# First expert stage of a decoder layer: the gate-weighted one-hots of the first key are built on GpSimd instead of VectorE

## The reference, cut to what matters

```python
q = jnp.einsum('td,dhq->thq', xt, w_pq)                # 8 heads, two halves of 128
v1, i1 = lax.top_k(q[..., :half] @ keys1.T, 16)        # first key
v2, i2 = lax.top_k(q[..., half:] @ keys2.T, 16)        # second key
sc, ci = lax.top_k(v1[..., :, None] + v2[..., None, :], 16)
eid = i1[ci // 16] * 128 + i2[ci % 16]                 # 128 experts a token: 8 heads x 16
gate = softmax(sc)
hid = gelu(xt @ expert_u[eid])
out = (gate * hid) @ expert_v[eid]
```

## Time and profile before

| | |
|---|---|
| Median of 3 runs | 2118.77 us (2118.34 to 2120.36) |
| Span of the profiled execution | 2115.7 us |
| Median less span | 3.1 us |
| TensorE busy | 2016.0 us, 95% |
| VectorE busy | 1619.7 us, 77% |
| GpSimd busy | 552.0 us, 26% |
| Mean granted TensorE clock | 0.979 of full speed |

### The profile page before, as it was taken

How to read it: one execution, slowest core, us unless ns; L and a number is a source line. 1 busy time by engine, 2 the same in 40 slices (tenths; PEclk the granted TensorE clock), 3 DMA queues, 4 the chain that set the end, 5 groups by cost and what they waited for, 6 DMA issues and landing times.

```text
span 2115.7 us, 33945 instructions
## 1 busy us (share of the span) xinstructions
PE 2016.0 (95%) x12943; PEld 1845.7 (87%) x12943; DVE 1619.7 (77%) x3030; ACT 794.0 (38%) x1311; POOL 552.0 (26%) x334
## 2 busy tenths in 40 slices
PE   8998889889999999999999999999989899999998
PEld 8998879778756999999999999999978787778786
DVE  6635767564355327999999799999979888989888
ACT  4335453432331322322344444444433333333332
POOL 0000020000000000212112055555547656656540
PEclk9999889999999999999999999999999999999999
DMA  5223210151550403768667488999999999999993
GB/s 171 89 93 116 86 47 1 41 204 42 191 208 21 160 1 121 261 232 285 223 219 270 140 290 330 338 346 340 337 381 387 386 387 387 383 385 384 375 377 113
DMA packets 223185, 483.75 MB, mean 229 GB/s; under 512 B 11984, under 2 KB 137168, under 8 KB 221415
## 3 DMA queue, kind: packets, MB, share of 16 engines
q1 hardware_dynamic: 176998, 314.56, 41.9%
q0 software_dynamic: 46080, 167.79, 21.8%
HBM read 423.29 MB, written 58.36 MB: 228 GB/s over the span
## 4 chain that ended last, share of the span: by engine, by line
PE 43%; DMA 8%; DVE 5%; SPq 3%; issue 1%; ACT 1%; DVEq 0%; ACTq 0%
PE ps L2599 9%; PE ps L2595 9%; PE ps L2991 8%; PE ps L2594 8%; DMA raw_v<-peer_v 6%; PE ps L2585 5%; PE ps L2623 4%; SPq L2969 3%; DVE kept L3100 3%; DVE v_high_low L3163 1%; DVE outputs L3157 1%; DMA outputs<-hidden 1%; ACT v_high_low L3057 0%; DMA kept<-peer_v,kept 0%; SPq L2967 0%
## 5 line engine op out<-in xcount | busy, mean ns | idle before, releaser
L2991 PE MATMUL ps<-v_high_low,gated_high_low 128*128 128x512 f32 x2304 | 532.9, 393 | 22.0 <-ACT gated_high_low L3059 18.3
L2991 PEld LDWEIGHTS ps<-v_high_low,gated_high_low 128*128 128x128 f32 x2304 | 435.8, 190 | 119.0 <-ACT v_high_low L3057 15.0
L2594 PE MATMUL ps<-x_high_low,u_high_low 128*128 128x384 f32 x1024 | 356.3, 348 | 0.0
L2595 PE MATMUL ps<-x_high_low,u_high_low 128*128 128x384 f32 x1024 | 345.6, 337 | 0.0
L3083 POOL DMA_INDIRECT outputs<-peer_v,kept x138 | 264.2, 1914 | 170.0 <-DVE kept L3100 137.3
L2711 POOL DMA_INDIRECT scores<-peer_u,kept x64 | 94.0, 1468 | 729.3 <-DVE kept L2831 552.4
L2669 ACT ACTIVATE kept<-ps 128x384 f32<-128x384 f32 x128 | 62.9, 491 | 407.5 <-PE ps L2599 398.0
L2599 PE MATMUL ps<-x_high_low,u_high_low 128*128 128x384 f32 x1024 | 204.7, 341 | 0.0
L2595 PEld LDWEIGHTS ps<-x_high_low,u_high_low 128*128 128x128 f32 x1024 | 193.3, 189 | 0.0
L2594 PEld LDWEIGHTS ps<-x_high_low,u_high_low 128*128 128x128 f32 x1024 | 193.0, 189 | 0.0
L3163 DVE TENSOR_TENSOR v_high_low<-raw_v,v_high_low 128x1024 fp32r<-128x1024 f32 x120 | 146.3, 1219 | 51.1 <-ACT v_high_low L3057 51.1
(11 more groups left out here) (471 smaller groups left out, 4113.9 us busy)
## 6 DMA issues: line engine op xcount, KB each, us to landing
experts<-peer_u SPq DMA_DIRECT2D x63, 1024.0 KB
raw_v<-peer_v SPq DMA_DIRECT2D x60, 1024.0 KB
hidden<-kept SPq DMA_DIRECT2D x64, 384.0 KB
gates<-scores SPq DMA_DIRECT2D x12, 2048.0 KB, 9.4
first_hidden<-hidden SPq DMA_DIRECT2D x16, 768.0 KB, 18.4
outputs<-gates SPq DMA_DIRECT2D x16, 768.0 KB
outputs<-hidden SPq DMA_DIRECT2D x16, 768.0 KB, 15.4
first_gates<-gates SPq DMA_DIRECT2D x15, 768.0 KB
```

Of the source, the lines that this page charges most:

```text
L2594: pe.matmul(o, utr[:, b, HI, k], xr[:, HI, k, 0:DN], start=(k == 0), stop=False)
L2595: pe.matmul(o, utr[:, b, HI, k], xr[:, LO, k, 0:DN], start=False, stop=False)
L2991: ins = pe.matmul(bank(c, 2 * t + h), gr[:, slot, x, DN * b + P * t:DN * b + P * t + P], vr[:, slot, y, D * b + 512 * h:D * b + 512 * h + ...
```

## The change: what it does

The `gated` one-hots leave VectorE. GpSimd makes them, one token to an instruction: a `tensor_scalar` of 128 x 128 elements that compares the row of key numbers with the token's first keys and multiplies by the token's gates, both taken as one value per partition. That is 8 instructions for each octet, 384 in all, where VectorE had 2 for each octet, 96 in all. VectorE keeps the one comparison for `hot2`. TensorE waits for both before an octet's first call. GpSimd's gathers are no longer asked for as soon as the ring allows: ahead of octet `o` it asks for those that the ring allows after the dot products of octet `o - 2`. The number of dot products that VectorE makes after octet `o` now comes from `dots_after(o)`, which rounds down where the old expression rounded up.

```diff
+OCTETS = NTG * QG // 2
+
+def dots_after(o):
+
+    return DOTS_BY[2] if o < 0 else min(ROWSETS, DOTS_BY[2] + (ROWSETS - DOTS_BY[2]) * (o + 1) // (OCTETS + 3))
...
                 if first == 0:
                     pe.wait_ge(hot_set, tg * (QG // 2) + (i // 2 + 1))
+                    pe.wait_ge(gated_hot_set, tg * (QG // 2) + (i // 2 + 1))
...
-            for no in range(ROWSETS):
-                i = no % RING
-                if no == PAIRS_EACH:
-                    pool.wait_ge(ids_set, 2)
-                after(pool, row_used, no - RING + 1)
-                pool.indirect_dma_start(out=ring[i], out_offset=None, in_=d.peer_u[0],
-                                        in_offset=bass.IndirectOffsetOnAxis(ap=ids[:, no:no + 1], axis=0)).then_inc(row_in[i], 16)
+            asked = [0]
+
+            def gather(upto):
+                for no in range(asked[0], min(upto, ROWSETS)):
+                    i = no % RING
+                    if no == PAIRS_EACH:
+                        pool.wait_ge(ids_set, 2)
+                    after(pool, row_used, no - RING + 1)
+                    pool.indirect_dma_start(out=ring[i], out_offset=None, in_=d.peer_u[0],
+                                            in_offset=bass.IndirectOffsetOnAxis(ap=ids[:, no:no + 1], axis=0)).then_inc(row_in[i], 16)
+                asked[0] = max(asked[0], min(upto, ROWSETS))
+
+            gather(DOTS_BY[2] + RING)
+            pool.wait_ge(gates_set, 1)
+            for o in range(OCTETS):
+                gather(dots_after(o - 2) + RING)
+                slot = o % 2
+                after(pool, made, 2 * (o - 1))
+                for t in range(OCT):
+                    at, cols = OCT * o + t, slice(P * t, P * t + P)
+                    ins = pool.tensor_scalar(gated[slot][:, cols], iota, kt[:, 0, at:at + 1], kt[:, 3, at:at + 1], ALU.is_equal, ALU.mult)
+                ins.then_inc(gated_hot_set, 1)
+            gather(ROWSETS)
...
-            before, octets = dots[0], NTG * QG // 2 + 3
-            for o in range(NTG * QG // 2):
+            for o in range(OCTETS):
                 t0, slot = OCT * o, o % 2
                 after(v, made, 2 * (o - 1))
-                keys, k2 = over(iota, 1, [P, OCT, NK]), hot2[slot].rearrange("p (t k) -> p t k", t=OCT)
-                k1 = gated[slot].rearrange("p (t k) -> p t k", t=OCT)
-                v.tensor_tensor(k1, keys, over(kt[:, 0, t0:t0 + OCT], 2, [P, OCT, NK]), ALU.is_equal).then_inc(hot_first, 1)
-                v.tensor_tensor(k2, keys, over(kt[:, 1, t0:t0 + OCT], 2, [P, OCT, NK]), ALU.is_equal)
-                v.wait_ge(hot_first, o + 1)
-                v.tensor_tensor(k1, k1, over(kt[:, 3, t0:t0 + OCT], 2, [P, OCT, NK]), ALU.mult).then_inc(hot_set, 1)
+                v.tensor_tensor(hot2[slot].rearrange("p (t k) -> p t k", t=OCT), over(iota, 1, [P, OCT, NK]),
+                                over(kt[:, 1, t0:t0 + OCT], 2, [P, OCT, NK]), ALU.is_equal).then_inc(hot_set, 1)
                 if lows[0] < NK:
                     low()
-                while dots[0] < min(ROWSETS, before - (before - ROWSETS) * (o + 1) // octets):
+                while dots[0] < dots_after(o):
                     dot()
```

More of the change, by code:

```diff
@@ L2503, in phase_hidden @@
         "tile_picked", "pairs_turned", "pairs_turned_out", "gate_exps", "gate_sums", "gates_set"))
-    hot_set, hot_first, made, gkept = s("gated_one_hots_set"), s("first_one_hots_set"), s("gates_made"), s("gates_kept")
+    hot_set, gated_hot_set, made, gkept = s("one_hots_set"), s("gated_one_hots_set"), s("gates_made"), s("gates_kept")
     xs_in, ids_set, exp_s, gelu_s = s("sample_x_in"), s("expert_ids_set"), s("gathered_gate_exps"), s("gathered_gelu")
```

## The result

The changed kernel takes 2317.19 us (median of 4 runs, 2315.87 to 2324.20) against 2118.56 us for the kernel before (4 runs, 2118.05 to 2120.36). The ratio is 1.0943, with a 95% interval of 1.0927 to 1.0959: 9.4% slower. The profiled execution took 2315.87 us, with a span of 2314.1 us against 2115.7 us, 198.4 us more. Forecast were 2121 us, within 2113 to 2208.

The account below looks back on a forecast made before the run. TensorE was taken to set the pace at 6.87 us a row; 2115.7 - 0 + 0 + 2.4 = 2118.1 us of span, with 3.1 us between span and median 2121 us, 0.1% over before. The range was 2113 to 2208 us.

Parts of the forecast that it names:

- So 0.31 us is the work and the rest is waiting: GpSimd's 128-column additions in another stage, shown as 0.90 and 0.78 us: 0.31 us work, the rest waiting for VectorE.
- eight are 2.7 us: GpSimd's eight one-hots of an octet, at 0.34 us each, take 2.7 us a row.
- the additions show next to no fixed cost: Argument against dearer one-hots: GpSimd's additions take 1.27 us for 512 columns and 0.31 for 128.
- The sum for GpSimd's row: Gathers 3.96 us plus one-hots 2.7 us make 6.7 us a row, under TensorE's 6.87 by 0.2 us.
- The first octet: Tightest octet: between gates set and TensorE taking it, 5.2 us are left for 2.7 us of one-hots.
- The prediction is wrong if GpSimd's row passes 6.87 us: Stated condition for failure: GpSimd's work per row exceeds TensorE's row of 6.87 us; equality at 0.36 us for each one-hot.
- A one-hot costs more than 0.36 us: Rival, 29%: dearer one-hots on GpSimd give 2152 us at 0.45 us each, 2208 at 0.60, 2276 at 0.78.
- Turns: Rival, 21%: GpSimd shut out during VectorE's three two-input instructions, 3.42 us; its row 8.0 us, total 2175 us.
- The rule that speaks against it: VectorE instructions with two SBUF inputs and GpSimd instructions reading SBUF exclude each other; the prediction charged this only to gathers.
- Three of its four instructions a row can be held up by one one-hot each: VectorE's instructions held by GpSimd's one-hots: 3 x 0.34 = 1.0 us a row, out of 2.3 us of slack.
- VectorE's relief: Two instructions a row off VectorE, 109 us in all, lie beside TensorE, which never waits for them; counted 0.
- The rounding at the stage's end: Dot products rounded down start the last gather 4.7 us later; next stage up to 3.3 us late, 2.4 us taken.

Follow-up runs that it names:

- cols64: The changed kernel with gated one-hots of 64 columns instead of 128 from the third octet on, part of the result left out; 2244.44 us.
- tiny_dots: The changed kernel with the dot products of the stretch shortened to 16 elements, most of each left out; 2238.27 us.
- split4: The changed kernel with GpSimd making four of an octet's eight gated one-hots and VectorE the others, whole result computed; 2187.68 us, ratio 1.0318.
- light_before: The kernel before without VectorE's multiplication of the one-hots by the gates, nothing in its place; 2121.37 us, ratio 1.0007.
- split2_up: The changed kernel with two of an octet's one-hots on GpSimd, six on VectorE, and dot products rounded up as before; 2117.63 us, ratio 0.9997.
- low_halves: The changed kernel with VectorE's low part cut in two halves and a dot product between them, whole result computed; 2309.55 us, ratio 1.0900.
- split3_up: The changed kernel with three of an octet's one-hots on GpSimd, five on VectorE, and dot products rounded up as before; 2141.07 us, ratio 1.0096.

## Why the prediction was wrong, by its own steps

**"So 0.31 us is the work and the rest is waiting": this step failed.** The term "eight are 2.7 us" measured 8 x 0.79 = 6.3 us. The stated upper bound, the shorter row of 0.78 us in the earlier trace rows taken whole, was the right price almost to the digit. It had been argued away by a reading of turns with an estimate in it (0.55 us for each VectorE addition) and by "the additions show next to no fixed cost". That last claim rested on the same reading: 0.31 us was the result of it, not a second piece of evidence. `cols64` puts the fixed cost of this instruction at 0.34 us.

One more view of the kernel before bears on the turns of the earlier trace rows. The first line is GpSimd, the others are VectorE:

```profile
309.66 1.26 POOL L1520 TENSOR_TENSOR layer<-layer,kept 128x512 f32<-128x512 f32 x1 [3.30 <-DVE layer L1415]
309.70 1.37 DVE L1412 TENSOR_TENSOR layer<-layer,kept 32x128 f32<-32x128 f32 x1
...
316.76 0.69 DVE L1425 TENSOR_TENSOR layer<-layer,kept 128x512 f32<-128x512 f32 x1 [3.09 <-PE ps L1139]
```

VectorE's small addition of L1412 ends 0.15 us after GpSimd's, and the two of L1425 that take 2.07 us in the earlier trace rows take 0.69 us each when GpSimd is idle. So there VectorE was held as well. But what is left of a GpSimd row once VectorE has ended, 0.31 us, is not its price: what passes while it is held isn't in it. The held one-hots of the changed kernel show that. They end 0.50 to 0.67 us after VectorE's run, where a free one takes 0.79. What an addition of 128 columns costs alone stands in no trace.

**The sum for GpSimd's row.** 6.7 us had been reckoned and 10.8 measured. The one-hots were 3.6 us too low. The gathers were 1.2 us too high: 2.3 + 0.4 = 2.7 us with their gaps, not 3.96, since VectorE is idle for long once TensorE waits. Holding of one-hots, charged at nothing, is 1.75 us. 6.7 + 3.6 - 1.2 + 1.75 = 10.85, against 10.87 us for TensorE's row. Over the 6.87 us of before it is (10.87 - 6.87) x 47 = 188 us. The first octet adds 3.5 us of waiting and the end of the stage 3.5, together 195 of the 198.4 us of the span. VectorE's idle time as the reason for the shorter gathers is argued from its 224 us of work in 521.

**The condition was right.** "The prediction is wrong if GpSimd's row passes 6.87 us", and its margin was 0.2 us with the price of eight instructions unknown. Eight times an unknown between 0.16 and 0.78 us spans 5 us a row. The middle of that span, 0.47 us, already lies above the 0.36 us at which the row no longer fits, which the chances (45% for the forecast) did not reflect.

**The rivals.** Both came true, and at once. "A one-hot costs more than 0.36 us" had at 0.78 us 2276 us as its end. "Turns" had a row longer by 3.42 us at most from holding. They were given as cases that exclude each other, so no number stood for the two together, and the range was cut at 2208 us inside the first. By the prediction's own terms the two together are 3.42 + 2 x 0.94 + 8 x 0.78 = 11.5 us a row, near the 10.9 measured. (The times of the dearer one-hot were also added to 2119 us and not to the forecast's 2121, which makes them 2 us too low.) `tiny_dots` (2238 us, with little holding left) and `split4` (2188 us, where only holding passes the limit) show each of them by itself.

**The rule that speaks against it** was right and was charged in too few places. The Trainium skill ("SBUF — State Buffer", section on who interferes with whom) says that such a VectorE instruction and a GpSimd instruction that reads SBUF exclude each other for their whole length. One-hots of 3.72 us beside such instructions, and of 0.79 us beside the low part with its operand in PSUM (62 of them in the changed kernel, none over 0.81 us), agree. The runs differ from the rule in two ways. A one-hot is mostly held through a whole run of such instructions, 1.63, 2.82 and 3.72 us for one, two and three. And VectorE hardly waits when it is the second to start. In the changed kernel:

```profile
1253.87 0.79 POOL L2733 TENSOR_SCALAR one_hots<-kept,experts 128x128 f32<-128x128 f32 x1
1253.94 1.44 DVE L2755 SCALAR_TENSOR_TENSOR scores<-scores,kept 128x1024 f32<-128x1024 f32 x1
```

Shut out until the one-hot had ended, the dot product would have taken 0.72 us more than its 1.22; it took 0.22 us more. "Three of its four instructions a row can be held up by one one-hot each" was thus nearly the wrong way round: 136 of these 147 VectorE instructions keep their 1.22 us, the other 11 take at most 1.45 us, and GpSimd pays nearly all.

**Steps that held.** TensorE set the pace and VectorE's relief is worth nothing (`light_before`, and `split2_up` with 6 of 8 tokens left on VectorE). The rounding at the stage's end costs time, with the right mechanism: 3.5 us in the changed kernel, 5.4 alone, where 2.4 was taken and 3.3 was the limit. The places named for a wrong price and for turns are those where the trace shows them: one-hots far apart with VectorE idle, long ones beside the dot products, TensorE waiting ahead of L2630.

**The first octet** was said to have 5.2 us for 2.7. It needed 8.7 us for eight one-hots: 6.3 by the same price and 2.4 of holding. TensorE waited 3.35 us for it.

## What to carry to other kernels

Work that moves to an idle engine has to fit its budget per period there; multiply its number of instructions by a price that was measured for that very kind, and if the price is only bounded, forecast from the bounds and not from the best reading inside them. In these runs GpSimd paid an estimated 0.34 us for each small instruction before its first column, and paid again when VectorE read two SBUF operands beside it; its free places were those in which VectorE was idle or read PSUM. An engine that is full but waited for by nobody gives nothing back when it is relieved, and rivals that can come together have to be priced together.

## What the runs showed of the hardware that was not expected

- A `tensor_scalar` of GpSimd with two values per partition takes 0.78 us at 128x128 and 0.56 us at 128x64; with constants 0.68 us, with one operation and one value 0.58 us, each with VectorE idle.
- A one-hot is held through a run of VectorE instructions with two SBUF operands, and VectorE hardly is: 11 of 147 such instructions in the changed kernel and 26 of 149 in `low_halves` took more than 1.24 us, the longest 1.45 and 1.52 us. In the earlier trace rows, where GpSimd adds two tensors, VectorE was held for longer: 1.37 us for an addition of 32x128.
- What lets GpSimd in stays open. In the changed kernel three held one-hots came free after two instructions of a run of three (the one from 1319.38 us took 2.88 us and ended 0.65 us after the third had begun). In `split3_up` the held one-hot ended (1358.55) before VectorE's run was over.
- The octets that are caught follow a pattern: all the loss lies in one of the two buffers (1.24 against 0.79 us). In `low_halves` most of it moved to the other buffer (1.13 against 0.84 us), and in `split3_up` both have it (1.52 and 1.45 us). So the buffer itself isn't the cause; what fixes the pattern is not shown.
- The granted clock of TensorE was 0.86 on average in the stretch in which it waited, between its levels of 1.2 and 2.4 GHz, against 1.00 in the earlier trace rows. It can have cost little: GpSimd was busy for 496 of the 521 us and never waited for TensorE there.
